# Stacked operands in the recurrent stage and paired score products: 23 products for each chunk and head in place of 31

## The reference, cut to what matters

```python
def step(S, inp):
    r_t, w_t, k_t, v_t, a_t, b_t = inp
    sa = jnp.einsum('bhij,bhj->bhi', S, a_t)
    S = S * w_t[:, :, None, :] + sa[..., None] * b_t[:, :, None, :] + v_t[..., None] * k_t[:, :, None, :]
    return S, jnp.einsum('bhij,bhj->bhi', S, r_t)
...
    sc = (jnp.einsum('bqhd,bkhd->bhqk', q_nope[:, s:e], k_nope[:, :e])
          + jnp.einsum('bqhr,bkr->bhqk', q_rope[:, s:e], k_rope[:, :e])).astype(jnp.float32) * scale
```

## Time and profile before

| | us |
|---|---|
| median of 3 runs (2678.49 to 2692.53) | 2684.79 |
| the profiled execution's own time | 2680.27 |
| its span | 2678.4 |
| PE busy, whole span | 2269.2 |
| DVE, POOL, ACT busy, whole span | 1329.1, 1204.5, 785.0 |
| the recurrent stage's passes, from the first product to the last y sum | 541 to 1319 |
| latent attention, heads | some 1650 to 1950 |

### The profile page before, as it was taken

The page is one execution under the profiler, slowest core; times in us unless marked ns, Lnnn a source line. Parts: engine busy times, 40 slices in busy tenths (PEclk is TensorE's granted clock), DMA queues, the critical chain, the costliest instruction groups (busy, mean ns, idle before and its releaser), DMA issues.

```text
span 2678.4 us, 66254 instructions
## 1 busy us (share of the span) xinstructions
PE 2269.2 (85%) x26582; PEld 1966.0 (73%) x26582; DVE 1329.1 (50%) x1923; ACT 785.0 (29%) x1899; POOL 1204.5 (45%) x708
## 2 busy tenths in 40 slices
PE   6799999978877777878594999999988599798776
PEld 4698998977777777777594895777778476576555
DVE  7666666644544444444525531444422443638655
ACT  1623323324433333433312122333311212211331
POOL 1466666531312213122584680222177588775235
PEclk8899999999999999999697999999989799999998
DMA  2234334331212112120221221000013121121001
GB/s 82 88 134 163 145 138 162 136 144 31 81 43 82 43 48 77 43 82 21 103 97 39 71 87 55 32 31 31 16 59 120 45 94 55 63 79 55 24 0 63
DMA packets 66813, 198.41 MB, mean 74 GB/s; under 512 B 26784, under 2 KB 29088, under 8 KB 62240
## 3 DMA queue, kind: packets, MB, share of 16 engines
q1 hardware_dynamic: 66592, 195.24, 21.0%
HBM read 156.24 MB, written 38.99 MB: 73 GB/s over the span
## 4 chain that ended last, share of the span: by engine, by line
PE 57%; issue 9%; DVE 6%; ACT 2%; POOL 2%; POOLq 1%; DVEq 0%; ACTq 0%
PE wide L771 18%; PE wide L1175 8%; PE wide L1176 8%; PE wide L1177 8%; PE wide L1651 4%; PE wide L1747 2%; PE wide L1711 2%; PE wide L1712 1%; PE wide L1536 1%; PE wide L1731 1%; PE wide L1999 1%; DVE normed L1313 1%; PE wide L2225 1%; DVE inv_rms L1300 1%; ACT odd_probs L2242 1%
## 5 line engine op out<-in xcount | busy, mean ns | idle before, releaser
L1038 POOL TENSOR_TENSOR n_levels<-n,masks 128x192 f32<-128x192 f32 (+1 forms) x96 | 115.4, 1215 | 548.7 <-ACT n L918 548.7
L1175 PE MATMUL wide<-mixed_high,w_high_rwkv_in 128*128 128x264 f32 x720 | 213.0, 296 | 28.0 <-ACT log_decay L435 19.0
L1177 PE MATMUL wide<-mixed_high,w_low_rwkv_in 128*128 128x264 f32 x720 | 207.3, 288 | 0.0
L996 DVE TENSOR_TENSOR x_w<-wide,x_w 128x384 f32<-128x384 f32 (+1 forms) x176 | 95.9, 545 | 187.2 <-PE wide L771 180.5
L1176 PE MATMUL wide<-u_low_second,w_high 128*128 128x512 f32 x464 | 186.2, 401 | 0.0
L1199 POOL TENSOR_TENSOR w_high<-weights,con 128x1024 fp32r<-128x1024 f32 x60 | 147.5, 2458 | 75.9 <-PE wide L1177 66.0
L1292 DVE TENSOR_TENSOR sq_sum<-sq_sum,squares 128x528 f32<-128x528 f32 (+1 forms) x54 | 87.3, 1617 | 180.9 <-ACT squares L1257 180.9
L355 PE MATMUL wide<-mixed_in,weights 128*128 128x264 f32 x672 | 158.6, 394 | 13.8 <-DVE mixed_in L325 12.3
L1175 PEld LDWEIGHTS wide<-mixed_high,w_high_rwkv_in 128*128 128x128 f32 x720 | 138.8, 193 | 36.4 <-ACT log_decay L435 25.2
L1202 POOL TENSOR_TENSOR w_low<-weights,w_high 128x1024 fp32r<-128x1024 f32 x60 | 157.7, 2628 | 4.7
L355 PEld LDWEIGHTS wide<-mixed_in,weights 128*128 128x128 f32 x672 | 128.8, 193 | 41.1 <-issue 9.5
(11 more groups left out here) (322 smaller groups left out, 6878.6 us busy)
## 6 DMA issues: line engine op xcount, KB each, us to landing
weights<-in_stream SPq DMA_DIRECT2D x200, 512.0 KB, 3.5
forms<-form SPq DMA_DIRECT2D x16, 2020.5 KB, 6.3
forms_in<-forms SPq DMA_DIRECT2D x16, 1440.0 KB, 7.0
gate_bonus<-forms SPq DMA_DIRECT2D x16, 576.0 KB, 4.0
r_of_pair<-forms SPq DMA_DIRECT2D x16, 288.0 KB, 3.9
mixed<-gate_bonus SPq DMA_DIRECT2D x14, 264.0 KB, 2.1
gated<-mixed SPq DMA_DIRECT2D x14, 264.0 KB, 5.9
x<-in_tokens SPq DMA_DIRECT2D x4, 528.0 KB, 5.0
```

The costliest lines, as they stand in the source:

```text
L996: dve.tensor_tensor(both, inv_bank[g][:, 0:2 * n].rearrange("p (s n) -> p s n", s=2)[:, :, 0:m], both, ALU.add).then_inc(q["xw_added"], 1)
L1038: return pool.tensor_tensor(n_lvl[:, first:last, grp(g), :], n_all[:, grp(g), :].unsqueeze(1).to_broadcast([P, n, GC, C]), b_con[:, 1 + fi ...
L1175: pe.matmul(dst, w[0], x[0], start=start, stop=False)
L1177: return pe.matmul(dst, w[1], x[0], start=False, stop=stop)
```

## The change

In the recurrent stage three pairs of things are kept side by side and used as one operand. b and k of a chunk stand beside each other, and G becomes one product with 128 columns of weights (b and k) against a, r and the unit matrix: it gives what G, K and the turned b and k gave. N becomes one product with a and v as weights against the unit matrix and b, and gives the turned v and a too. Its result is 128 rows. u stands over v (u in one half of the partitions, v in the other), and the turned b over the turned k, so that one product over 128 rows gives the state's new part, and one gives y's. Old state against a and r is one product with 128 columns of weights. So a chunk and head takes 23 products in place of 31. Products with 64 rows and 128 columns now alternate with products of 64x64 and of 128 rows and 64 columns.

What comes with it: the items `rows` and K are gone, G is five items of two chunks with ten mask operations of DVE, ACT copies per head (two copies for u, two for y, four for an N group), the last chunk's state is not made, `forms_in` comes in eight DMAs, `r` in two, three masks and two copies of the unit matrix are set up ahead, semaphore instructions of their own before PE's items are gone, and the first walk item stands behind the first G.

In the latent attention the rotated query is written to both halves of the partitions, so that the k_rope products of two score blocks can be issued as 64-row products in different halves, one after the other: the two halves of the last block's keys, and blocks 2 and 3. Blocks 0 and 1 use a copy of the rotated key with zeros in its lower half. The order of the products and of the three signals changes.

```diff
-        qg, mg = sbb("b_with_a_r", 2, NC, 2, C), sbb("k_with_a_r", 2, NC, 2, C)
-        v_tok, k_tok, b_tok = (sbb(n, 2, NC, C) for n in ("v_rows_rwkv", "k_rows", "b_rows"))
-        state, state_p, u_row, eye = (sbb(n, C) for n in ("state", "state_decayed", "u_rows", "eye"))
+        AR_EYE, ROWS = 3, 2
+        V_LOWER, A_AT, V_UPPER, R_AT, SPARE, EYE_AT, OWN, CROSS, BLOCKS_IN = range(9)
+        FORMS_GAP, SCAN_GAP = 120, 48
+
+        b_k = sbb("b_and_k", 2, 2, NC, AR_EYE, C)
...
+        b_f = sbb("forms_in", 2, NC, BLOCKS_IN, C)
...
+        r_a_r = sbb("r_ahat_r", 2, NC, 3, C)
...
+        uv = sbb("u_and_v", 2, 2, NC, C)
...
-        state_bank, chunk_bank, y_bank = wide[2][:, 0, :], wide[2][:, 1, :], wide[3][:, 0, :]
+        state_bank = wide[2][:, 0, :]
+        out_bank = [wide[2][:, 1, :], wide[3][:, 0, :]]
...
         def sp_forms(sp, i, par_, reused):
 
             if reused:
-                wait_heads(sp, token_mm, 12 * (i - 1))
-            sp.dma_start(b_f[:, par_, :], forms[i, :, 0:5 * LP]).then_inc(forms_loaded[par_], 16)
+                wait_heads(sp, g_mm, NC * (i - 1))
+                sp.sem_inc(q["turn"], 1)
+            loaded, to = forms_loaded[par_], b_f[:, par_]
+
+            def form_of(rows, at):
+                return forms[i, rows, at:at + LP].rearrange("p (c n) -> p c n", c=NC)
+
+            for part, block in enumerate((A_AT, R_AT)):
+                sp.dma_start(to[:, :, block, :], ar_of(i)[:, :, part, :]).then_inc(loaded, 16)
+            for rows, v_to, b_to, k_to in ((UPPER, V_UPPER, OWN, CROSS), (LOWER, V_LOWER, CROSS, OWN)):
+                for at, block in ((F_B, b_to), (F_K, k_to), (F_V, v_to)):
+                    sp.dma_start(to[rows, :, block, :], form_of(rows, at)).then_inc(loaded, 16)
...
+            for rows, slot in ((UPPER, 2), (LOWER, 0)):
+                sp.dma_start(r_a_r[rows, par_, :, slot, :], ar_of(i)[rows, :, 1, :]).then_inc(scan_loaded[par_], 16)
...
-                for g in range(GROUPS):
-                    rest += [("G", g, 6), ("N", g, 3)]
-                rest += [("start", g, 0) for g in range(GROUPS)]
-                rest += [("rows", n, 3) for n in range(3)] + [("K", g, 6) for g in range(GROUPS)]
-                filler += [("M", g, 3) for g in range(GROUPS)] + [("rows", n, 3) for n in range(3, 12)]
+                rest += [("G", 0, 6), ("N", 0, 6), ("G", 1, 6), ("start", 0, 0), ("N", 1, 6), ("G", 2, 6), ("start", 1, 0), ("N", 2, 6),
+                         ("G", 3, 6), ("G", 4, 3), ("start", 2, 0)]
+                filler += [("M", g, 3) for g in range(GROUPS)]
...
-                v = v_tok[:, pw, c, :]
-                out_u, out_s, out_y = (bank[:, 0:C] for bank in (chunk_bank, state_bank, y_bank))
+                block = slice(0, C)
                 if part == 0:
+                    if p > 0 or c > 0:
+                        pe.wait_ge(q["y_rows"], 2 * (NC * p + c))
                     if c == 0:
                         wait_scan(pe, p, pw)
                         pe.wait_ge(q["a_rows"], GROUPS * i)
-                        if not is0(p):
-                            pe.wait_ge(q["y_rows"], 9 * p)
-                            pe.wait_ge(q["s_rows"], 9 * p)
                     else:
-                        pe.wait_ge(q["y_rows"], 9 * p + c)
-                    begin()
-                    by_head(out_u, xw[:, W_OF + pw, c * C:(c + 1) * C], mv[:, pw, c, :], True, c == 0, u_mm if c == 0 else None)
-                    by_head(out_y, mg[:, pw, c, 1, :], v, True, False)
-                    if c > 0:
-                        pe.wait_ge(q["s_rows"], 9 * p + c)
-                        begin()
-                        by_head(out_u, a_hat[:, pw, c, :], state, False, True, u_mm)
-                        by_head(out_y, b_r[:, pw, c, :], state, False, False)
-                    by_head(out_s, k_tok[:, pw, c, :], v, True, False)
+                        pe.wait_ge(q["s_rows"], (NC - 1) * p + c)
+                        for hd, rows in enumerate(HEAD_ROWS):
+                            pe.matmul(out_bank[hd][:, block], r_a_r[rows, pw, c, 1 - hd:3 - hd, :], state[rows], start=True, stop=False)
+                    for hd, rows in enumerate(HEAD_ROWS):
+                        pe.matmul(out_bank[hd][rows, block], xw[rows, W_OF + pw, c * C:(c + 1) * C], mv[rows, pw, c, :],
+                                  start=c == 0, stop=True).then_inc(u_mm[hd], 1)
                 else:
-                    pe.wait_ge(q["u_rows"], 9 * p + c + 1)
-                    begin()
-                    by_head(out_s, b_tok[:, pw, c, :], u_row, False, True, s_mm)
-                    by_head(out_y, qg[:, pw, c, 1, :], u_row, False, True, y_mm)
...
+                    for n, c in enumerate(two_chunks(arg)):
+                        for hd, rows in enumerate(HEAD_ROWS):
+                            form, width = b_f[rows, par_, c], AR_EYE * C
+                            pe.matmul(b_k_bank(arg, hd)[:, n * width:(n + 1) * width], form[:, OWN:CROSS + 1, :], odd_blocks(form, A_AT, EYE_AT),
+                                      start=True, stop=True).then_inc(g_mm[hd], 1)
...
+                    for n, c in enumerate(range(NC)[grp(arg)]):
+                        upper, lower = (b_f[rows, par_, c] for rows in HEAD_ROWS)
+                        a_v = (upper[:, A_AT:V_UPPER + 1, :], lower[:, V_LOWER:A_AT + 1, :])
+                        eye_b = (upper[:, EYE_AT:OWN + 1, :], odd_blocks(lower, EYE_AT, CROSS))
+                        for hd in range(2):
+                            mm = pe.matmul(odd_bank[hd][:, n * 2 * C:(n + 1) * 2 * C], a_v[hd], eye_b[hd], start=True, stop=True)
+                            if n == GC - 1:
+                                mm.then_inc(n_mm[hd], 1)
...
-                    wait_heads(act, u_mm, 9 * p + c + 1)
-                    act.activation(u_row[:], chunk_bank[:, 0:C], ACT.Copy).then_inc(q["u_rows"], 1)
+                    for hd, rows in enumerate(HEAD_ROWS):
+                        act.wait_ge(u_mm[hd], NC * p + c + 1)
+                        act.activation(uv[rows, pw, hd, c, :], out_bank[hd][rows, 0:C], ACT.Copy).then_inc(q["u_rows"], 1)
                 else:
-                    wait_heads(act, y_mm, 9 * p + c + 1)
-                    act.activation(y_rows[:, pw, c, :], y_bank[:, 0:C], ACT.Copy).then_inc(q["y_rows"], 1)
+                    for hd, rows in enumerate(OTHER_ROWS):
+                        act.wait_ge(y_mm[hd], NC * p + c + 1)
+                        act.activation(y_rows[rows, pw, c, :], out_bank[hd][rows, 0:C], ACT.Copy).then_inc(q["y_rows"], 1)
...
+                    for hd, rows in enumerate(HEAD_ROWS):
+                        act.wait_ge(n_mm[hd], GROUPS * i + arg + 1)
+                        act.activation(n_all[rows, grp(arg), :], with_rows(hd)[rows, :, 1, :], ACT.Copy).then_inc(q["n_rows"], 1)
+                    for hd in range(2):
+                        act.activation(uv[:, par_, hd, grp(arg), :], with_rows(hd)[:, :, 0, :], ACT.Copy).then_inc(q["v_rows"], 1)
...
+                    chunks = two_chunks(arg)
+                    n, width = len(chunks), AR_EYE * C
+                    for hd in range(2):
+                        dve.wait_ge(g_mm[hd], NC * i + chunks[-1] + 1)
+                        dve.tensor_tensor(b_k[:, par_, hd, chunks[0]:chunks[-1] + 1, :, :].rearrange("p c s n -> p c (s n)"),
+                                          b_k_bank(arg, hd)[:, 0:n * width].rearrange("p (c n) -> p c n", c=n),
+                                          b_k_mask[:, hd].rearrange("p s n -> p (s n)").unsqueeze(1).to_broadcast([P, n, width]),
+                                          ALU.mult).then_inc(q["b_k_made"], 1)
...
+                    for hd, rows in enumerate(HEAD_ROWS):
+                        dve.tensor_tensor(xw[rows, W_OF + par_, flat(arg)].rearrange("p (c n) -> p c n", c=GC), b_k[rows, par_, hd, grp(arg), 0, :],
+                                          eye[rows].unsqueeze(1).to_broadcast([C, GC, C]), ALU.add).then_inc(q["w_start"], 1)
...
+            for hd, rows in enumerate(HEAD_ROWS):
+                other = OTHER_ROWS[hd]
+                dve.tensor_copy(b_k_mask[rows, hd, 0, :], b_con[rows, LEVEL0T, :])
+                dve.tensor_copy(b_k_mask[other, hd, 0, :], b_con[other, STRICT, :])
+                dve.tensor_copy(b_k_mask[:, hd, 1, :], b_con[:, INCLUSIVE, :])
+            dve.memset(b_k_mask[:, :, ROWS, :], 1.0)
+            dve.wait_ge(q["eye_set"], 1)
+            for par_ in range(2):
+                dve.tensor_copy(b_f[:, par_, :, EYE_AT, :], eye[:].unsqueeze(1).to_broadcast([P, NC, C])).then_inc(q["eye_set"], 1)
+            dve.drain()
...
             for own, rows in zip(q_rope_of, HEAD_ROWS):
-                dve.tensor_tensor(own[rows, :], q_rope[rows, :], sq[rows, 0, :], ALU.add).then_inc(e["rope"], 1)
+                for half in HEAD_ROWS:
```

(34 more changed lines are left out.)

212 lines of the change are left out of this document (106 added, 106 removed).

## The result

The changed kernel takes **2554.28 us** (median of 4 runs, 2551.5 to 2557.2) where the kernel before, run beside it, takes 2684.3: a ratio of 0.951, with a 95% interval of 0.949 to 0.954. It is 53 us faster than the 2607 that I forecast and inside the range, but it lies in the first rival's band (2480 to 2570) and not in that of my own case (2585 to 2630). The profiled execution took 2552.2 us with a span of 2549.9; before it was 2680.27 and 2678.4, so the two traces differ by as much as the runs do.

What follows compares the result with a forecast made beforehand. PE was taken as held by instruction-fetch stops in the recurrent passes and by its own work in attention. From 2680.27: passes -75, bare walk +3, set-up +3, attention -9 give 2602; median 4.5 above: 2607 us (range 2525 to 2705).

Steps and rivals of the forecast that it cites:

- first rival: Recurrent passes: fetch stops vanish while DVE and ACT keep up, 36.6 us a pass; 2510 us, chance 0.17.
- my own case: Whole kernel: a recurrent pass falls 4.7 us to 42.7; 2607 us, own range 2585 to 2630, chance 0.43.
- The fetch term: Recurrent pass: PE's stops for instruction blocks fall from 8.6 to 3.6 us, between 6.4 (stop unchanged) and 0.7 (hidden).
- Products: Recurrent pass: PE's products, those left and those stacked, take 26.8 us against 33.3 before.
- The second rival: State and y: the two heads' products over 128 rows don't overlap, plus 24 us; 2631 us, chance 0.15.
- Changes of shape: Recurrent pass: 38 changes of tile shape on PE cost 0.095 us each, 3.6 us.
- Waits: Recurrent pass: new PE waits, 2.2 for DVE, 0.2 for ACT's N copies, 0.8 in the walk; 3.2 us.
- old rest of 5.5: Recurrent pass before the change: waits, half clock and starts beside products and fetch stops, 5.5 us, kept in the forecast.
- Fixed parts: Outside the sixteen inverse passes: set-up copies on DVE before the first G plus 3 us, bare walk of pass 16 plus 3.
- The part with the attention: Latent attention: paired score products save 0.70 us a head, 11 over 16; some becomes waits, minus 9 (bounds 0, 11).
- New waits: Recurrent passes: waits for DVE, ACT and POOL reach 8 us for 3.2, plus 77; 2684 us, no change, chance 0.13.
- Tiles in turn: Recurrent stage and attention: stacked tiles sharing all columns don't run side by side, 47.8 us a pass; 2700 us, chance 0.12.

Runs made afterwards that it cites:

- e1: The kernel before, with only the stand-alone semaphore instruction ahead of each PE item deleted, its waits standing on the products: 2548.4 us.
- e3: The kernel before, with every product of E streaming its 64 columns twice, same number of instructions: 2661.3 us, ratio 0.994.
- e2: The changed kernel, with a stand-alone semaphore instruction put back ahead of each PE item: 2601.0 us.
- e7: The changed kernel, with the last N group moved behind G 3, G 4 and the last start: 2522.8 us.
- e10: The kernel before, with two stand-alone semaphore instructions ahead of each PE item in place of one: 2711.7 us.
- e8: The changed kernel, with the old state's product cut into two of 64x64 for each head: 2528.3 us.

## Why the prediction came out as it did

**The bound was read rightly.** PE waiting for its instructions was the largest idle time, and the time came from there: e1 and the missing row "issue" show it. (Eight of the 58 stops that the prediction priced weren't fetches, as said above; the size of the term, 68.5 us, hardly moves by it.)

**The fetch term is the one that failed**: I took 3.6 us a pass, "the middle" between 6.4 and 0.7, and 0.5 was left. That is 3.1 x 16 = 50 of the 53 us. Two steps in it were wrong. The middle was taken without a row for it: heavier blocks do hide fetches (e3), and with `begin` left in they alone bring the stops to 1.4 us (e2), near my lower bound. That is 2.2 of the 3.1. The other 0.9 is the step that treated the semaphore instructions as mere filling of a block ("semaphore instructions fill the rest"): in the kernel before, they were what made a fetch stop PE (e1). The measured 2601 us of e2, beside a forecast of 2607 that took no account of their going, is partly luck: its stops are 2.2 us a pass under the forecast, and the products below 1.3 over it.

**Products: 26.8 forecast, about 28 measured.** G came as forecast and N 0.04 over it, as PE in order of time shows beside the earlier trace rows (three products of N, two of G for both heads):

```profile
853.39 0.94 PE L865 MATMUL wide<-forms_in 64*128 64x128 f32 x12
854.16 0.82 PE L853 MATMUL wide<-forms_in 64*128 64x192 f32 x8
...
856.00 0.94 PE L865 MATMUL wide<-forms_in 64*128 64x128 f32 x12 [0.64 <-ACT u_and_v L960]
856.77 0.82 PE L853 MATMUL wide<-forms_in 64*128 64x192 f32 x8
857.42 0.34 PE L812 MATMUL wide<-state,r_ahat_r 64*128 64x64 f32 x4
```

N: 0.77 / 3 = 0.26, with or without a wait ahead of it, for 0.22 (plus 0.3 a pass); G: 0.65 / 2 = 0.32. The old state was mis-sized, 0.28 for 0.22 (plus 0.5 a pass). State and y over 128 rows do overlap; PE in order of time in the changed kernel:

```profile
876.97 0.34 PE L820 MATMUL wide<-u_and_v,b_and_k 128*64 128x64 f32 x4
877.14 0.29 PE L823 MATMUL wide<-u_and_v,b_and_k 128*64 128x64 f32 x4
877.36 0.56 PE L797 MATMUL wide<-x_w,e 64*64 64x64 f32 x12
```

The two take 0.39 us with one change of shape, so 0.15 each for both heads (forecast 0.117, in turn 0.233): plus 0.5, and 28.1 in all. The second rival is out. The rule of the Trainium skill that stood behind it (TensorE: Matmul & The Clock Gate, Part 3, "The mechanism": a weight load overlaps only if its row group differs) isn't borne out here, where the tiles share all rows and differ in columns.

**Changes of shape: 0.095 forecast.** From 877.14 to 877.36 there are 0.22 us, 0.09 more than the 0.13 of these products' own pitch, and the trace has 38 changes a pass. As forecast.

**Waits: 3.2 new ones forecast.** What a pass has beside products, changes of shape and stops is 39.9 - 28 - 3.6 - 0.5 = 7.8 us, for 8.7 forecast. The place was right (masks and starts of DVE, ACT's copies for N and u: 37.0 us in the six rows of waits, 4.6 a pass, for 2.2 before). What I didn't foresee is that an idle stretch there also costs the clock, nor POOL beside the starts; e7 shows the two are worth 2.3 us a pass, so the term came out right in sum partly by luck. A second part of the luck: the old rest of 5.5 was carried over whole, though the change drops 58 semaphore records a pass, some 1.5 us at e10's 25 ns (an estimate).

**Fixed parts.** Set-up (plus 3) can't be told apart in the trace: the first centring comes 11.5 us earlier, after the first passes' gain. The bare walk of pass 16 took 32.2 us between the last two centrings, 32.0 before: plus 0.2, for plus 3. The part with the attention gave 12.6, for 9, give or take what that part varies by: my upper bound of 11 for the products was the whole of it (0.7 a head, as computed), and next to nothing turned into waits.

**The other rivals.** New waits took (4.6 - 2.2) x 16 = 38 us, not 8 a pass. Tiles in turn are excluded by every pair above. The rival "only the fetch counts" had the stops right and DVE wrong.

**What stays open.** How a semaphore instruction delays a fetch. The runs show that one ahead of an item does it, a second adds next to nothing to the stops, moving it ahead of the waits takes a quarter away, and the effect comes one to two blocks late. They don't show what starts a fetch. Nor was it tried whether another light instruction in its place would do the same.

## What to carry to other kernels

When PE stops "by issue" between the records of one product, look first for stand-alone semaphore instructions in its stream, and put the increments and waits on products: here one deleted line gave 127 us, 4.7%, at no cost. Before crediting a large rewrite with its gain, run its smallest part alone; the stacking here, without that line, was worth nothing until its order and one product were mended (2554 to 2501 us). What held it back was the one product with more columns of weights (128) than it streams (64): cut in two it was 26 us faster (e8).

## What the runs showed of the hardware

- 85 stand-alone semaphore instructions more a pass cost 25 ns each on average (e10); the first of an item moreover exposes instruction fetches, 8.6 against 0.55 us a pass without it (e1). Without them this trace agrees with the Trainium skill (Runtime: NRT & Kernel Launch, "Instruction fetch mechanics") that a fetch is mostly hidden; with them it doesn't.
- A pair of products with 128 columns of weights and 64 streamed took 0.28 us; the same work as four tiles of 64x64 took 0.16, and a pair of these 0.117.
- Two tiles over the same 128 rows and different 64 columns ran side by side, 0.15 us for both.
- Two additions of 64x192 on DVE took 3.74 us beside POOL's products of 128x768, 1.0 to 1.1 beside its products of 128x192, and 0.73 with POOL idle (e7).
- PE, with 12 MATMUL records from 860 to 862 us, fell to 1.2 GHz in the window from 862 to 864, and was still there in the one from 870 to 872, fully busy since 868. In e7, as empty from 845 to 847, it stayed at 2.4 GHz through the next two windows.
